# Norm sums as token columns, roots on 128x4 spread by TensorE, and shared keys and values from an unscaled input

## The reference, cut to what matters

```python
def rmsnorm(x, w):
    xf = x.astype(jnp.float32)
    y = xf * lax.rsqrt(jnp.mean(xf * xf, axis=-1, keepdims=True) + EPS)
    return (y * w.astype(jnp.float32)).astype(x.dtype)

def shared_kv(x, kv_norm, kv_w, kv_b_f):
    h = rmsnorm(x, kv_norm)
    proj = h @ kv_w
    k, v, f = jnp.split(proj, [D_MODEL, 2 * D_MODEL], axis=-1)
    ...
    log_f = jax.nn.log_sigmoid(f.astype(jnp.float32) + kv_b_f.astype(jnp.float32))
    c = jnp.cumsum(log_f, axis=1).transpose(0, 2, 1)
    return k, v, c
```

## Time and profile before

| what | value |
|---|---|
| median of 3 runs | 2815.42 us (2811.32 to 2817.82) |
| the profiled execution | 2819.05 us, its span 2817.2 us |
| TensorE busy | 96% of the span, 12374 matmul instructions |
| weight loads busy | 75% |
| VectorE, ScalarE busy | 55%, 36% |
| mean granted clock of TensorE | 0.973 |
| HBM read | 262.72 MB |

### The profile page before, as it was taken

How to read it: one execution, slowest core, us unless ns; L and a number is a source line. 1 busy time by engine, 2 the same in 40 slices (tenths; PEclk the granted TensorE clock), 3 DMA queues, 4 the chain that set the end, 5 groups by cost and what they waited for, 6 DMA issues and landing times. The chain is left out here.

```text
span 2817.2 us, 31111 instructions
## 1 busy us (share of the span) xinstructions
PE 2704.8 (96%) x12374; PEld 2105.5 (75%) x12374; DVE 1537.9 (55%) x2571; ACT 1023.0 (36%) x1555; POOL 99.5 (4%) x124
## 2 busy tenths in 40 slices
PE   6999999999999999999998999899999998999998
PEld 4877688887976656888876876688887764688886
DVE  4455676876245553747465245466653798434332
ACT  3344443333234444434245234333222213323322
POOL 0000001000000000000000000011100010000000
PEclk9999999999799999999999999999999899999999
DMA  4322335553121102333324210266652120233331
GB/s 137 105 90 76 89 98 172 157 157 112 47 88 47 38 23 75 105 90 105 90 75 132 76 60 16 75 194 194 193 151 82 38 60 30 75 97 97 97 97 45
DMA packets 282967, 266.84 MB, mean 95 GB/s; under 512 B 13267, under 2 KB 268551, under 8 KB 282823
## 3 DMA queue, kind: packets, MB, share of 16 engines
q1 hardware_dynamic: 266759, 210.47, 24.3%
q0 software_dynamic: 15024, 54.33, 6.5%
q10 hardware_dynamic: 1040, 0.07, 0.0%
HBM read 262.72 MB, written 2.10 MB: 94 GB/s over the span
## 5 line engine op out<-in xcount | busy, mean ns | idle before, releaser
L445 DVE TENSOR_TENSOR w_lo<-raw,w_hi 128x1024 fp32r<-128x1024 f32 x396 | 484.5, 1227 | 785.0 <-ACT w_hi L440 784.0
L2044 PE MATMUL G<-H_hi,w_hi 128*128 128x512 f32 (+1 forms) x2016 | 811.7, 403 | 15.1 <-DVE H_lo L342 7.9
L440 ACT ACTIVATE w_hi<-raw 128x1024 fp32r<-128x1024 f32 x396 | 417.7, 1057 | 1072.3 <-PE G L2044 953.5
L2044 PE MATMUL G<-H_lo,w_hi 128*128 128x512 f32 (+1 forms) x2016 | 787.7, 391 | 0.0
L2044 PE MATMUL G<-H_hi,w_lo 128*128 128x512 f32 (+1 forms) x2016 | 787.7, 391 | 0.0
L2044 PEld LDWEIGHTS G<-H_hi,w_hi 128*128 128x128 f32 x2016 | 382.3, 190 | 133.6 <-issue 53.5
L2044 PEld LDWEIGHTS G<-H_lo,w_hi 128*128 128x128 f32 x2016 | 382.5, 190 | 82.8 <-issue 7.9
L2044 PEld LDWEIGHTS G<-H_hi,w_lo 128*128 128x128 f32 x2016 | 382.0, 189 | 80.5
L2044 PE MATMUL G<-hid_hi,w_hi 128*128 128x512 f32 x864 | 342.3, 396 | 4.7 <-DVE hid_lo L550 4.7
L2044 PE MATMUL G<-hid_lo,w_hi 128*128 128x512 f32 x864 | 337.7, 391 | 0.0
L2044 PE MATMUL G<-hid_hi,w_lo 128*128 128x512 f32 x864 | 337.7, 391 | 0.0
(11 more groups left out here) (282 smaller groups left out, 2603.5 us busy)
## 6 DMA issues: line engine op xcount, KB each, us to landing
raw<-in_w_ff SPq DMA_DIRECT2D x128, 512.0 KB
mod_w<-in_w_mod POOLq DMA_DIRECT2D x96, 512.0 KB, 4.5
raw<-in_ffn_w_up SPq DMA_DIRECT2D x176, 256.0 KB
raw<-in_ffn_w_down SPq DMA_DIRECT2D x40, 512.0 KB
raw<-in_w_in SPq DMA_DIRECT2D x28, 512.0 KB
raw<-in_mlstm_w_in SPq DMA_DIRECT2D x24, 512.0 KB
raw<-in_kv_w SPq DMA_DIRECT2D x16, 512.0 KB
raw<-in_fox_w_qg SPq DMA_DIRECT2D x16, 512.0 KB
```

The source lines that it names most:

```text
L440: act.activation(w_hi[:, j, :], raw[:, j, :], ACT.Copy).then_inc(hi_done, 1)
L445: dve.tensor_tensor(w_lo[:, j, :], raw[:, j, :], w_hi[:, j, :], ALU.subtract).then_inc(lo_done, 1)
L2044: mm = pe.matmul(G[:, 2 * p + m, 0:n], lw[:, k, ms], rh[:, t, 0:n], start=(t == 0 and q == 0), stop=(t == st["ktiles"] - 1 and q == 2), sk ...
```

## The change

Fourteen of the norms (all but ctx, `BY_COLUMN`) are summed with the squares stationary, a block of 128 tokens at a time, and one column of `ones` moving: the sums come out as 128x4, tokens on the partitions. Ln and Exp work on 128x4 into `col`. TensorE then makes the row of roots again: for each of the four blocks it takes the column, repeated 128 times, as stationary operand and the identity as moving one (`spread`), into M[:, 1]. VectorE reads the row there; for ffn0, kv and ffn1 (`KEPT_ROWS`) ScalarE copies it to `root` first. The spread is issued right behind the sums, and in ffn0, ffn1 and kv inside the second group of the projection. The kv stage works on X unscaled in the manner of ffn0: its sums and half of the modulation's columns for layer 0 are issued through `need` in kv_v's first group, the values are scaled by ScalarE when they are read (a scale for each token, four pieces of 128x256 instead of one of 128x1024), the keys by VectorE instead of a copy by ScalarE, and the gates' row by VectorE ahead of the bias. The mean in the conformer is made in the same way: six tiles' sums move behind the taps, two stay, and the mean is spread.

```diff
+            if name in BY_COLUMN:
+                act.activation(col[:], M[:, 0, 0:TB], ACT.Ln, bias=eps[:, 0:1], scale=1.0 / D).then_inc(n_sd, 1)
+                act.wait_ge(n_sd, i + 1)
+                act.activation(col[:], col[:], ACT.Exp, scale=-0.5).then_inc(n_col, 1)
+                return
...
+        def keep_row_act(act, name):
+            act.wait_ge(n_kept, KEPT_ROWS[name] + 1)
+            act.activation(root, M[:, 1, :], ACT.Copy).then_inc(n_row, 1)
...
+            def column_sums(c, src, first, last):
+                for b in range(TB):
+                    mm = pe.matmul(M[:, 0, c + b:c + b + 1], src[:, b * P:b * P + P], ones[:, 0:1], start=(first and b == 0),
+                                   stop=(last and b == TB - 1), skip_group_check=True)
+                return mm
+
+            def spread(src):
+                for b in range(TB):
+                    mm = pe.matmul(M[:, 1, b * P:b * P + P], src[:, b:b + 1].to_broadcast([P, P]), ident[:],
+                                   start=(b == 0), stop=(b == TB - 1), skip_group_check=True)
+                return mm
+
+            def root_row(name):
+                pe.wait_ge(n_col, BY_COLUMN[name] + 1)
+                spread(col).then_inc(n_kept if name in KEPT_ROWS else n_row, 1)
...
-                        pe.matmul(M[:, 0, :], ones[:], SQ[:, m, :], start=(start and m == 0),
-                                  stop=(g == 3 and m == 1),
-                                  skip_group_check=True).then_inc(n_ss, 1)
+                        column_sums(0, SQ[:, m, :], start and m == 0, g == 3 and m == 1).then_inc(n_ss, 1)
...
+                if g >= 2:
+                    column_sums(4, Y[:, g - 2, :], g == 2, False)
...
-            for t in range(DT):
+            for t in (6, 7):
                 pe.wait_ge(cv_d, t + 3)
-                mm = pe.matmul(M[:, 1, :], ones[:], Y[:, t, :], start=(t == 0), stop=(t == 7))
-            mm.then_inc(cv_s, 1)
+                mm = column_sums(4, Y[:, t, :], False, t == 7)
+            mm.then_inc(cv_c, 1)
+            pe.wait_ge(cv_b, 1)
+            spread(mean).then_inc(cv_s, 1)
...
+                    if part == 0:
+                        for _ in range(5):
+                            next(up)
+                        root_row(f"ffn{layer}")
+                    finish(up)
...
-            mod_columns(pe, 0, 0, 20)
-            norm("kv", between=lambda t: mod_columns(pe, 0, 20 + 3 * t, 23 + 3 * t))
-            mod_columns(pe, 0, 44, 64)
-            linear("kv_v", H_hi, H_lo, "T", need=from_h("kv"))
+            root_row("fpost0")
+            mod_columns(pe, 0, 0, 32)
+
+            def kv_need(t):
+                mod_columns(pe, 0, 32 + 4 * t, 36 + 4 * t)
+                norm_tiles("kv", (t,))
+                pe.wait_ge(h_lo, FILL["kv"] + t + 1)
+
+            kv_values = linear_units("kv_v", H_hi, H_lo, "T", need=kv_need)
+            for _ in range(5):
+                next(kv_values)
+            root_row("kv")
+            finish(kv_values)
...
-            norm_act(act, "kv", X, x_from("fpost0"))
-
+            unscaled_act(act, "kv", "fpost0", kv_weight, used_after("f0_up2"))
+            act.wait_ge(n_col, BY_COLUMN["kv"] + 1)
+            act.activation(root_T[:], col[:], ACT.Copy, scale=0.5).then_inc(root_c, 1)
+            keep_row_act(act, "kv")
...
+            def keys_out(i, p, g):
+                dve.tensor_tensor(two(xK, g), G[:, 2 * p:2 * p + 2, :], root.unsqueeze(1).to_broadcast([P, 2, T]),
+                                  ALU.mult).then_inc(pair_read[p], 1)
```

More of the change, by code:

```diff
@@ L118 @@
 NORM = {name: i for i, name in enumerate(NORMS)}
+BY_COLUMN = {name: i for i, name in enumerate(n for n in NORMS if n != "ctx")}
+KEPT_ROWS = {name: i for i, name in enumerate(("ffn0", "kv", "ffn1"))}
 RESIDS = {"post0": 8, "fpost0": 16, "post1": 24, "fpost1": 32}
-READY = {name: 8 * i for i, name in enumerate(f for f in FILLS if f not in ("mlstm", "fox", "mix", "conf", "ffn0", "ffn1"))}
+READY = {name: 8 * i for i, name in enumerate(f for f in FILLS if f not in ("mlstm", "fox", "mix", "conf", "ffn0", "ffn1", "kv"))}
 HIDDEN = {"f0": 0, "f1": 22, "s0": 44, "s1": 60}
@@ L173, in build @@
         sel_x = small("sel_x", [16, 16], F32R)
+        root_T = small("root_T", [P, TB])
+        col = small("col", [P, TB])
+        mean = small("mean", [P, TB])
         stat = small("stat", [P, 8, 8])
@@ L1105, in fox_act @@
             act.wait_ge(mod_s, 1)
[L1106 to L1109, removed]
+            keys = group_steps(act, "kv_k", split_hi, None)
             next(keys)
@@ L2106, in norm_tiles @@
                         pe.wait_ge(n_sd, i)
-                    pe.matmul(M[:, 0, 0:blocks * P], ones[:], squares[:, t % 2, 0:blocks * P], start=(t == 0),
-                              stop=(t == 7)).then_inc(n_ss, 1)
+                    if name in BY_COLUMN:
+                        mm = column_sums(0, squares[:, t % 2, :], t == 0, t == 7)
+                    else:
+                        mm = pe.matmul(M[:, 0, 0:blocks * P], ones[:], squares[:, t % 2, 0:blocks * P], start=(t == 0),
+                                       stop=(t == 7))
+                    mm.then_inc(n_ss, 1)
             def gate_rows(n, width, t):
@@ L2175, in _ @@
             fox_pe(pe, linear, linear_units, from_h, squares_behind)
+            root_row("post1")
             ffn1(1)
-            second_pe(pe, linear, linear_units, norm, from_h, squares_behind)
+            root_row("fpost1")
+            second_pe(pe, linear, linear_units, norm, root_row, column_sums, spread, from_h, squares_behind)
         @block.scalar
@@ L2209, in _, with kv_values_out @@
                           allow_slow_non_contiguous=True).then_inc(g_dma, 16)
-            fill_act(act, "kv", None, None, used_after("f0_up2"))
+            def kv_values_out(i, p, g):
+                act.wait_ge(root_c, 1)
+                for b in range(TB):
+                    one = act.activation(xV[:, b, g * GC:g * GC + GC], tokens_out(p)[:, b], ACT.Copy,
+                                         scale=root_T[:, b:b + 1])
+                one.then_inc(pair_read[p], 1)
+            kv_steps = group_steps(act, "kv_v", split_hi, kv_values_out)
+            next(kv_steps)
+            next(kv_steps)
+            next(kv_steps)
             gate_weights_act(act, 1)
-            plain(act, "kv_v", lambda g: xV[:, :, ds(g * GC, GC)], tokens_out, ACT.Copy, 0.5)
+            finish(kv_steps)
             fox_act(act)
```

108 lines of the change are left out of this document (67 added, 41 removed).

## The result

The changed kernel takes **2879.35 us** (median of 4 runs, 2875.03 to 2880.79) where the kernel before takes 2813.37 (median of 4, 2810.72 to 2817.82): a ratio of 1.0229, 95% interval 1.0211 to 1.0246. It is slower by 66 us; the forecast was +83 (2899), in a range of 2845 to 2935. The two profiled executions lie 56 us apart (2819.05 and 2875.03), because the one of after was the fastest of its four and the one of before lies above all four of its.

What follows compares the result with a forecast made beforehand. TensorE, busy 96% of the span, and its clock level were taken as the bound. Terms of 3 + 6.8 + 6.8 + 36.8 + 8.5 + 21.5 = 83.4 us on 2815.4 gave 2899 us, range 2845 to 2935.

Steps and rivals of the forecast that it cites:

- Sums as columns: Norm sums on TensorE: 0.90 us a tile at full clock, 1.70 at low, so no gain; 3 us in all.
- Rival 4: Column sums spaced 0.031 us an instruction, so a tile costs 0.25 us instead of 0.86: 2778 us; 4%.
- Roots and spreading: Path from sums to VectorE: 1.9 us at full clock, 2.8 at low, instead of 1.42; two sums of 6.8 us.
- fpost0 and kv: From fpost0's root to the gate rows: clock falls, modulation columns and first tiles run low; +8.5 us, between 7 and 10.
- pre0, even, conf: Norms where TensorE has only sums: low clock and longer root path cost 6.5, 6.5 and 8.5 us, sum 21.5.
- ffn0, ffn1: Norms between projection tiles: all eight tiles stay at the low clock, 4.27 us each; 18.4 us each, 36.8 together.
- rival 1: The clock comes back early in the ffn stages: loss 53.6 us, total 2869 us; 20%.
- mlp0: A norm where everyone waits for the root: the longer root path at low clock costs 1.4 us.
- Rival 3: Column sums inside projections also make the clock fall: up to 41 us more, 2920 us for half, 2940 for all; 10%.
- rival 5: ScalarE's wait behind the kept row reaches TensorE as a late weight split: some us in each of three stages; 4%.
- Rival 2: The clock goes as before everywhere and only latencies stay: 16 us, total 2832 us; 12%.

Runs made afterwards that it cites:

- run 9: The changed kernel with every spread of a root issued twice into the same place: 2901.23 us, ratio 1.0300.
- Run 1: The kernel before with unscaled keys and values and only the kv norm summed in columns, all else in rows: 2814.21 us, ratio 1.0001.
- run 2: Layer 0's modulation columns woven into the values' projection: with rows and unscaled keys/values 2809.51 us, in the changed kernel 2869.78, in the kernel before 2808.80.
- run 4: The changed kernel with pre0, even, conf and the convolution's mean summed in rows again: 2849.23 us, ratio 1.0130.
- run 5: The changed kernel with rows again in the eight norms behind a projection's pairs: 2845.33 us; in another kernel, rows again in ffn0 and ffn1: 2870.64 us.
- runs 6, 7: First, the changed kernel repeated for a second profile: 2879.52 us; second, the changed kernel with each tile's sum columns in ffn0 and ffn1 issued twice: 2897.05 us.
- run 8: The changed kernel with the old 512-column row product added before each tile's columns in pre0, even and conf, its result unread: 2907.27 us, ratio 1.0314.

## Why the prediction was right, and where not

- **Sums as columns** held: 0.107 to 0.113 us an instruction at the full level (0.95 us for eight, the last one's end included) and 0.213 at the low one, so no gain at either. Rival 4 (0.031 us an instruction) is out.
- **Roots and spreading** held to a tenth of a microsecond: VectorE starts 2.70 to 2.86 us behind the sums at the low level in every norm that waits, against 2.8. By run 9 the spreads are a third of the loss or a little more.
- **fpost0 and kv**: 7.7 us in the profile, forecast 8.5, by the route described: columns at 0.50, tiles 4.05 us apart at first. Run 1 shows that the unscaling by itself is worth nothing, as forecast, and run 2 why.
- **pre0, even, conf**: forecast 21.5, in the profile 26.5, by run 4 30 us with the mean. pre0 came out at 6.1 (its terms 4 + 1.4 + 0.8 add to 6.2, not 6.5), even at 7.7 for 6.5, mean and conf at 8.9 for 8.5. The rest is a term that the forecast put at nothing: it took the column sums of Y in the convolution's groups as free, because TensorE and VectorE had ended there within 0.27 us of each other. They cost 0.85 us a group, 3.8 us up to the last group's start; without them (run 4) the groups are back at their old distance.
- **ffn0, ffn1** is the step that failed: 36.8 us forecast, 1.9 in the first profile, 5 by the stages of twelve profiles, 9 by the medians of run 5. The step said that a mix of columns and products does not bring the clock back, by its nearest row, 697.5:723.2, a mix of columns with sums of 0.85 us. Six long products a tile are another mix, and the clock came back after one to four tiles (runs 6, 7). This is rival 1, which had 20%, and its 2869 is 10 us low. What brings the clock back in one mix and not in the other stays open (run 8).
- **mlp0** took 6.0 us where 1.4 were forecast. Run 1, which has row sums there, is 4.7 us slower in that stage than the profiled execution of before, too: most of it is a fall of the clock near 1760 us in the attention that the profile of before happened to escape, and not the change's. Behind that fall, from the start of the even layer's output projection to the first up projection, the kernels with columns take 53.6 us and those with rows 50.6 to 52.4, so the share of the change is 1.2 to 3.0, for 1.4.
- **Rival 3** (pairs inside projections make the clock fall) and **rival 5** (a wait of ScalarE that reaches TensorE) did not occur: no wait of TensorE for a weight split stands in the list, and the pairs run at 1.84 us for sixteen.
- **Rival 2** (the clock as before everywhere) is out: there are 112 us more at the low level.
- A slip without effect: the bound in rival 4 comes to (0.86 - 16/88)/8 = 0.085 us a column, not 0.082.

The forecast of the difference came out 17 us high (83 for 66): 28 to 32 too much in ffn, 8 to 9 too little in pre0, even, conf and the convolution, and the rest too little elsewhere, by 2 to 9 us as one takes the difference or run 5's 34 us (for 25 forecast with kv). So part of the closeness is luck: terms that were too small made up for a third or more of the one that was far too large.

## What to carry to other kernels

Count what a rewrite issues at TensorE, not the columns that it moves: eight f32 instructions with a full stationary load and one moving column take as long as two with 512, so that turning a sum by ones into columns saves nothing there, and a result that must return to all partitions by TensorE is a cost of its own (1 us at the full level, 2 at the low one). Where TensorE has nothing else to do, such columns double in price, because the clock falls beside them (13.8 us for 7.7 in conf); among long products most of them ran at the full level here, but they still cost their own time. What is put into a stage where TensorE never idles is paid in full, even where another engine used to end at the same time. And an operand left unscaled so that work can start early pays only if nothing already covers the wait: look at what stands over it first, and take that away in the same edit.

## What was not expected

- A stage's low-level time differs between executions of the same instructions by 6 us (95.9 and 102.0 in ffn0), enough to make a single profiled execution misleading for a term of a few us. A stage is better compared in several executions.
- In the same kernel the same mix, half of the time in 512-column products and half in columns, kept 1.00 through 14.2 us when it began there and 0.50 through 24 us when it began there (run 8), while six long products with eight or sixteen columns brought it back (runs 6, 7). What decides between these was not tried.
